# Summing the squares of a 2048-wide norm: from TensorE, group by group, to GpSimd in place with one product with the ones behind the last group

## The chip, the cores and the metric

The kernel runs on one core of a Trainium2 chip. The time is the device time of one execution in microseconds (us); the time before the change is 2414.93 us, the median of 3 runs (2414.13 to 2415.9). Everything is float32, and a float32 product takes two records of TensorE in the trace for each matmul of the code.

## The reference

Two layers of an encoder over 256 tokens of width 1024: differential attention and a bidirectional Mamba2 mixer beside each other, then a feed-forward part that fetches 128 experts' rows per token from HBM. The change touches one line of it, the norm behind the mixer (cut to what matters):

```python
y = (y_fwd + y_bwd + d_skip[:, None] * xs).reshape(b, s, SSM_INNER)   # SSM_INNER = 2048
return rmsnorm(y * jax.nn.silu(z), norm_g)          # then m @ w_ssm_br[l]

def rmsnorm(x, g):
    y = xf * lax.rsqrt(jnp.mean(xf * xf, axis=-1, keepdims=True) + RMS_EPS)
```

So the mean of the squares of 2048 features is wanted for each of 256 tokens.

## The kernel before

Each engine's program is written out by hand, in order, with semaphores between engines; no scheduler moves anything. In the stage that matters features lie on the 128 partitions and tokens along the free axis. The 2048 features are 16 tiles of 128 x 256, worked in 8 groups of two tiles, g = 0 to 7. For each group TensorE does, in this order: `beside(g + 1)`, half a chunk of the projection of z or of a gate (16 matmuls, L407); `c_times_b(g + 1)` (2 matmuls, L533); then, behind the semaphore `m_ready`, the 24 matmuls that give y of the group (L576); and from g = 2 on `sum_squares(g - 2)` (L554), two matmuls that multiply the squares with a 128 x 128 matrix of ones. They add up over the partitions, and over all 16 tiles in bank 7.

Beside it VectorE makes the differences of the decay matrices (L1166) and multiplies them with C times B (L1173 to L1182, which raises `m_ready`), adds the skip term to y and multiplies with silu(z) (L1189, L1194, which raises `yz_ready`), and scales z by the gain (L1199). ScalarE makes the exponentials (L821, L833), empties the half's bank (L815 or L794, in `aside`), and squares the group's two tiles with one instruction into `xbc` (L854, which raises `ysq_ready`), 512 elements on each partition. GpSimd only issues DMAs here: 16 loads of `fbuf`, two per group, into three slots (L1425). The load n is issued when the differences and the exponentials that used load n - 3 are done.

Behind the last group come `beside(9)`, the sums of groups 6 and 7, and the product of z with `w_ssm_br` (L392, 4 chunks of 32 matmuls each), which waits for three things: the chunk, the last scaling, and the last half's bank being emptied by ScalarE (`bank_empty`, L794). VectorE takes bank 7 (L1220), makes 1/rms of it with ScalarE's root (L875, L1224) and multiplies it into the second gates (L1225), which are first wanted when the first chunk's product is done (L1228). GpSimd's next work in the layer is fetching the experts' rows (L1443).

Of the kernel before, what the change touches and what calls it, by code (L numbers as in the profile page):

```python
# [16 lines left out]
ALU = mybir.AluOpType  # L17
# [3 lines left out]
DEPTH, SEQ, DM = 2, 256, 1024  # L21
# [8 lines left out]
XT = INNER // P  # L30
# [85 lines left out]
def encoder_kernel(nc, x, positions, consts, params, w_stream, w_dt, keys_t, norm2_rows, final_row,  # L116
                   peer_uv, out):
    with ExitStack() as ctx:
# [122 lines left out]
        def sem(name, per_layer):  # L241
            return Count(once(name), per_layer)
# [58 lines left out]
        ysq_ready = sem("ysq_ready", XT // 2)  # L301
        ysq_used = sem("ysq_used", XT // 2)
        yms_ready = sem("yms_ready", 1)
# [56 lines left out]
        def _(pe):  # L360
# [5 lines left out]
            for L in range(DEPTH):  # L366
# [183 lines left out]

                def sum_squares(g):
                    wait(ysq_ready, g + 1, L)
                    for u in range(2):
                        ins = pe.matmul(bank[7][:, 0:SEQ], ones, xbc[:, 2 * g + u, :],  # L554
                                        start=(g == 0 and u == 0), stop=(g == GROUPS - 1 and u == 1))
                    ins.then_inc(ysq_used.sem, 1)

                beside(0)
                for g in range(GROUPS):
# [19 lines left out]
                    ins.then_inc(y_done.sem, 1)  # L579
                    if g >= 2:  # L580
                        sum_squares(g - 2)
                beside(GROUPS + 1)
                sum_squares(GROUPS - 2)
                sum_squares(GROUPS - 1)
                wait(m_scaled, GROUPS, L)
# [378 lines left out]
        def _(dve):  # L964
# [32 lines left out]
            for L in range(DEPTH):  # L997
# [220 lines left out]

                wait(ysq_used, GROUPS, L)
                dve.tensor_scalar(r_bc[:], bank[7][:, 0:SEQ], 1.0 / INNER, EPS, ALU.mult, ALU.add)\  # L1220
# [184 lines left out]
        def _(pool):  # L1405
# [5 lines left out]
            for L in range(DEPTH):  # L1411
# [3 lines left out]
                pool.wait_ge(rows_stored.sem, rows_stored.at(L, 16))  # L1415
                wait(bank_full, M_ATT + 4, L)
                for n in range(F_UNITS):
                    g, d = divmod(n, 2)
                    if n >= 3:
                        gf, df = divmod(n - 3, 2)  # L1420
                        pool.wait_ge(diff_ready.sem, diff_ready.at(L, 4 * gf + 2 * df + 2))
                        pool.wait_ge(offexp_done.sem, offexp_done.at(L, 2 * gf + df + 1))
# [3 lines left out]
                                   rows_dram[L:L + 1, row:row + HPG, :].rearrange("o r t -> o (r t)")  # L1426
                                   .broadcast_to([P, HPG * TB * P])).then_inc(f_loaded[slot], 16)

                for p in range(TB * PARTS):
# [105 lines left out]
```

## Time and profile before

| | |
|---|---|
| median of 3 runs | 2414.93 us |
| the profiled execution: its time, its span | 2413.57 us, 2411.8 us |
| TensorE matmuls busy | 2081.5 us, 86% of the span |
| VectorE, ScalarE busy | 1327.4 us (55%), 749.5 us (31%) |
| the stage of the 8 groups | about 340 to 443 us in layer 0, 1534 to 1637 us in layer 1 |
| TensorE's granted clock in that stage | 1.00 of full speed |

The busy share of an engine is an average over stages with different limits; the chain of waits, cut to a stretch, says what ends last in that stretch. "PEld" is the loading of weights into TensorE, which runs ahead of the matmuls ("PE").

### The profile page before, as it was taken

Reading aid. Unit: us, or ns where it says so; the run is one execution under the profiler, and the core shown is the slowest. Engines: PE = TensorE matmul, PEld = TensorE weight load, DVE = VectorE, ACT = ScalarE, POOL = GpSimd, SP = SyncE. Lnnn points to the kernel's source line nnn. Section 1 sums busy time; section 2 is a strip of 40 time slices with the busy share of each in tenths; the row PEclk is TensorE's granted clock in tenths of the full one; section 3 lists DMA queues with packets and bytes.
Section 4 is the critical chain, followed back from the end, with each engine's and each line's share of the span. In section 5 each row is a group of like instructions: output and inputs, shape, how many; then the busy total and the mean of one; then the engine's idle time right before and its main releaser. Section 6 shows DMA issues by size and latency. Waiting matters only on the chain.

```text
span 2411.8 us, 23144 instructions
## 1 busy us (share of the span) xinstructions
PE 2081.5 (86%) x8312; PEld 1328.7 (55%) x8312; DVE 1327.4 (55%) x3225; ACT 749.5 (31%) x2017; POOL 513.4 (21%) x550
## 2 busy tenths in 40 slices
PE   5999999999878787777789999999998888777776
PEld 5688888866334332222276888888653344322322
DVE  1266458226657666765403772671366667666744
ACT  2034237103333233233220442570123332333232
POOL 0000000004334333333200000000133333333331
PEclk9999999999999999999999999999999999999999
DMA  4323444549999999999813234445499999999996
GB/s 155 135 105 140 156 172 163 201 165 373 422 422 421 422 421 421 421 421 421 370 70 134 111 140 167 166 158 201 178 387 421 421 421 421 421 422 421 422 421 268
DMA packets 90402, 705.31 MB, mean 292 GB/s; under 512 B 10000, under 2 KB 10128, under 8 KB 15792
## 3 DMA queue, kind: packets, MB, share of 16 engines
q0 software_dynamic: 78400, 553.81, 55.7%
q1 hardware_dynamic: 11168, 146.36, 15.8%
q10 hardware_dynamic: 720, 3.67, 0.5%
q8 instruction: 65, 1.06, 0.2%
q14 instruction: 49, 0.40, 0.0%
HBM read 702.62 MB, written 1.18 MB: 292 GB/s over the span
## 4 chain that ended last, share of the span: by engine, by line
PE 52%; DMA 32%; DVE 7%; ACT 4%; issue 2%; POOL 2%; SPq 0%; DVEq 0%; POOLq 0%; ACTq 0%
DMA ring<-in_peer_uv,ex_i 31%; PE bank L407 23%; PE bank L687 11%; PE bank L392 7%; DVE ring L1361 5%; PE bank L434 2%; POOL ring L1443 2%; PE bank L576 2%; PE bank L595 2%; PE bank L628 1%; ACT diag L926 1%; PE bank L554 1%; ACT wgt L919 1%; PE bank L481 1%; PE bank L533 1%
## 5 line engine op out<-in xcount | busy, mean ns | idle before, releaser
L687 PE MATMUL bank<-ring,diag 128*128 128x512 f32 x2048 | 949.7, 608 | 263.8 <-ACT diag L926 263.7
L1361 DVE SCALAR_TENSOR_TENSOR ring<-ring,h 128x1024 f32<-128x1024 f32 x512 | 607.1, 1223 | 478.4 <-DMA ring<-in_peer_uv,ex_i 478.4
L687 PEld LDWEIGHTS bank<-ring,diag 128*128 128x128 f32 x2048 | 373.2, 191 | 812.2 <-ACT diag L926 432.2
L1443 POOL DMA_INDIRECT ring<-in_peer_uv,ex_i x512 | 494.5, 966 | 1066.9 <-PE bank L687 686.3
L407 PE MATMUL bank<-hT,w_ring 128*128 128x256 f32 x2560 | 567.1, 381 | 1.9 <-ACT hT L718 1.9
L407 PEld LDWEIGHTS bank<-hT,w_ring 128*128 128x128 f32 x2560 | 485.1, 191 | 72.7 <-issue 5.3
L913 ACT ACTIVATE gel<-act_u 128x2 f32<-128x2 f32 x256 | 52.0, 203 | 854.9 <-DVE ring L1361 854.9
L926 ACT ACTIVATE diag<-cst,wgt 128x128 f32<-128x128 f32 x512 | 177.5, 394 | 25.8 <-PE bank L687 17.7
L919 ACT ACTIVATE wgt<-gel,gate_w 128x1 f32<-128x1 f32 x512 | 123.0, 287 | 9.3
L1414 POOL DMA_DIRECT2D cs_rows_dram<-cs_rows x2 | 1.3, 662 | 583.2 <-DVE cs_rows L1129 583.2
L1084 DVE SCALAR_TENSOR_TENSOR c_tmp<-xbc,par_all,c_tmp 128x254 f32<-128x254 f32 (+1 forms) x256 | 112.4, 481 | 4.5
L392 PE MATMUL bank<-zT,w_ring 128*128 128x256 f32 x512 | 110.8, 379 | 0.0
L392 PEld LDWEIGHTS bank<-zT,w_ring 128*128 128x128 f32 x512 | 97.3, 190 | 13.2
L1034 DVE TENSOR_TENSOR rot_tmp<-bank,sin_t 128x512 f32<-128x512 f32 x16 | 11.1, 692 | 142.8 <-PE bank L426 141.5
L628 PEld LDWEIGHTS bank<-hT,wq 128*128 128x128 f32 x512 | 60.0, 192 | 11.2 <-issue 9.2
L628 PEld LDWEIGHTS bank<-hT,w_ring 128*128 128x128 f32 x512 | 60.0, 192 | 8.6 <-issue 8.6
L1425 POOL DMA_DIRECT2D fbuf<-cs_rows_dram x32 | 17.4, 543 | 213.1 <-ACT m_mat L833 168.9
L628 PE MATMUL bank<-hT,wq 128*128 128x128 f32 x512 | 60.7, 276 | 1.6 <-ACT hT L882 1.6
L628 PE MATMUL bank<-hT,w_ring 128*128 128x128 f32 x512 | 60.1, 275 | 0.0
L1082 DVE TENSOR_SCALAR c_tmp<-xbc,par_all 128x256 f32<-128x256 f32 x64 | 23.4, 408 | 63.6 <-ACT xbc L767 63.6
L707 ACT ACTIVATE xn<-x_tok 128x1024 f32<-128x1024 f32 x10 | 10.5, 1051 | 153.4 <-DVE x_tok L1239 142.8
L392 PE MATMUL bank<-attT,w_ring 128*128 128x256 f32 x256 | 55.8, 380 | 2.4 <-ACT attT L805 2.4
(192 smaller groups left out, 1680.3 us busy)
## 6 DMA issues: line engine op xcount, KB each, us to landing
w_ring<-in_w_stream SPq DMA_DIRECT2D x62, 2048.0 KB, 8.3
fbuf<-cs_rows_dram POOLq DMA_DIRECT2D x32, 512.0 KB, 4.9
wq<-in_w_stream SPq DMA_DIRECT2D x4, 2048.0 KB, 8.2
ring<-in_peer_uv,ex_i POOLq DMA_INDIRECT x512, 14.5
out<-in_w_stream SPq DMA_DIRECT2D x2, 2048.0 KB, 12.2
keys<-in_keys_t ACTq DMA_DIRECT2D x2, 1024.0 KB, 4.9
x_tok<-in_x SPq DMA_DIRECT2D x1, 1024.0 KB, 5.1
g2row<-in_norm_rows ACTq DMA_DIRECT2D x2, 512.0 KB, 6.2
```

Of the source, the lines that this page charges most:

```text
L392: ins = pe.matmul(two(b0 + j // 2)[:, j % 2, :], w[:, k, j * P:(j + 1) * P], rhs(k), start=(k == 0), stop=(k == ks - 1))
L407: ins = pe.matmul(two(m % 2)[:, j % 2, :], w[:, k, j * P:(j + 1) * P], hT[:, k, :], start=(k == 0), stop=(k == KD - 1))
L434: ins = pe.matmul(bank[m % 2][:], hT[:, k, b * P:(b + 1) * P], w[:, k, :], start=(k == 0), stop=(k == KD - 1))
L576: ins = pe.matmul(two(5 + p)[u * SP_:(u + 1) * SP_, j, l * P:(l + 1) * P], xs[:, s, h * SP_:(h + 1) * SP_], m_mat[:, p, t, r, :], start=(n ...
L628: ins = pe.matmul(to[:, j * P:(j + 1) * P], w[:, k, j * P:(j + 1) * P], hT[:, k, b * P:(b + 1) * P], start=(k == 0), stop=(k == KD - 1))
L687: ins = pe.matmul(bank[b0 + n][:], diag[:, PAIR * (m % 2) + s, :], ring[:, slot, DM + n * 512:DM + (n + 1) * 512], start=False, stop=True, ...
L913: act.activation(gel[:, b, j:j + PAIR], act_u[:, b, j:j + PAIR], ACT.Gelu).then_inc(gelu_done.sem, 1)
L919: ins = act.activation(wgt[:, b, j + s:j + s + 1], gel[:, b, j + s:j + s + 1], ACT.Copy, scale=gates[:, j + s:j + s + 1])
L926: ins = act.activation(diag[:, PAIR * (m % 2) + s, :], ident, ACT.Copy, scale=wgt[:, b, j + s:j + s + 1])
L1084: ins = dve.scalar_tensor_tensor(out=dst, in0=src, scalar=w, in1=dst, op0=ALU.mult, op1=ALU.add)
L1361: ins = dve.scalar_tensor_tensor(out=row, in0=row, scalar=1.0, in1=h2[:, b, :], op0=ALU.mult, op1=ALU.mult, accum_out=act_u[:, b, PAIR * k ...
L1443: pool.indirect_dma_start(ring[:, PAIR * q + s, :], None, peer_uv, bass.IndirectOffsetOnAxis(ap=ex_i[:, b, j:j + 1], axis=0))\
```

## The change

Squares are no longer multiplied with the ones group by group. GpSimd adds the two tiles of squares of group g, as one instruction of 128 x 512, onto those of group 0, in place, for g = 1 to 7. The additions of groups 1 and 2 stand between its loads of `fbuf`, ahead of load 12 and of load 14; those of groups 3 to 7 behind the last load. TensorE multiplies the two summed tiles with the ones once, behind `beside(9)`, and waits for the seventh addition.

```diff
--- before.py
+++ after.py
@@ -299,7 +299,8 @@
         y_done = sem("y_done", GROUPS)
         yz_ready = sem("yz_ready", GROUPS)
         ysq_ready = sem("ysq_ready", XT // 2)
-        ysq_used = sem("ysq_used", XT // 2)
+        ysq_added = sem("ysq_added", GROUPS - 1)
+        ysq_used = sem("ysq_used", 1)
         yms_ready = sem("yms_ready", 1)
         yrms_ready = sem("yrms_ready", 1)
         m_scaled = sem("m_scaled", GROUPS)
@@ -548,13 +549,6 @@
                 def beside(n):
                     half(C_Z + 1 + n // 2, n % 2, M_Z + 2 + n)
 
-                def sum_squares(g):
-                    wait(ysq_ready, g + 1, L)
-                    for u in range(2):
-                        ins = pe.matmul(bank[7][:, 0:SEQ], ones, xbc[:, 2 * g + u, :],
-                                        start=(g == 0 and u == 0), stop=(g == GROUPS - 1 and u == 1))
-                    ins.then_inc(ysq_used.sem, 1)
-
                 beside(0)
                 for g in range(GROUPS):
                     p = g % 2
@@ -577,11 +571,11 @@
                                                     xs[:, s, h * SP_:(h + 1) * SP_], m_mat[:, p, t, r, :],
                                                     start=(n == 0), stop=(n == 2))
                     ins.then_inc(y_done.sem, 1)
-                    if g >= 2:
-                        sum_squares(g - 2)
                 beside(GROUPS + 1)
-                sum_squares(GROUPS - 2)
-                sum_squares(GROUPS - 1)
+                wait(ysq_added, GROUPS - 1, L)
+                for u in range(2):
+                    ins = pe.matmul(bank[7][:, 0:SEQ], ones, xbc[:, u, :], start=(u == 0), stop=(u == 1))
+                ins.then_inc(ysq_used.sem, 1)
                 wait(m_scaled, GROUPS, L)
                 wait(bank_empty, M_GSSM + 4, L)
                 for c in range(4):
@@ -1216,7 +1210,7 @@
                 scaled(GROUPS - 2)
                 scaled(GROUPS - 1)
 
-                wait(ysq_used, GROUPS, L)
+                wait(ysq_used, 1, L)
                 dve.tensor_scalar(r_bc[:], bank[7][:, 0:SEQ], 1.0 / INNER, EPS, ALU.mult, ALU.add)\
                     .then_inc(yms_ready.sem, 1)
                 wait(yrms_ready, 1, L)
@@ -1414,8 +1408,18 @@
                 pool.dma_start(rows_dram[L], cs_rows[0:2 * SH].rearrange("p b l -> p (b l)")).then_inc(rows_stored.sem, 16)
                 pool.wait_ge(rows_stored.sem, rows_stored.at(L, 16))
                 wait(bank_full, M_ATT + 4, L)
+                def add_squares(g):
+
+                    wait(ysq_ready, g + 1, L)
+                    if g > 1:
+                        pool.wait_ge(ysq_added.sem, ysq_added.at(L, g - 1))
+                    pool.tensor_tensor(xbc[:, 0:2, :], xbc[:, 0:2, :], xbc[:, 2 * g:2 * g + 2, :], ALU.add)\
+                        .then_inc(ysq_added.sem, 1)
+
                 for n in range(F_UNITS):
                     g, d = divmod(n, 2)
+                    if d == 0 and g >= 6:
+                        add_squares(g - 5)
                     if n >= 3:
                         gf, df = divmod(n - 3, 2)
                         pool.wait_ge(diff_ready.sem, diff_ready.at(L, 4 * gf + 2 * df + 2))
@@ -1425,6 +1429,8 @@
                     pool.dma_start(fbuf[:, slot].rearrange("p r b l -> p (r b l)"),
                                    rows_dram[L:L + 1, row:row + HPG, :].rearrange("o r t -> o (r t)")
                                    .broadcast_to([P, HPG * TB * P])).then_inc(f_loaded[slot], 16)
+                for g in range(3, GROUPS):
+                    add_squares(g)
 
                 for p in range(TB * PARTS):
                     b, c = divmod(p, PARTS)
```

TensorE's program of layer 0, in the middle of the loop (behind y of group 2; the names are the tiles that are written and read), before and after:

```order
L576 MATMUL bank<-m_mat,x_fwd 64x128 x2
L554 MATMUL bank<-xbc,cst 128x256 [waits ysq_ready]
L554 MATMUL bank<-xbc,cst 128x256
L407 MATMUL bank<-hT,w_ring 128x256 [waits bank_empty,chunk_loaded1]
L407 MATMUL bank<-hT,w_ring 128x256 x15
```

```order
L570 MATMUL bank<-m_mat,x_fwd 64x128 x2
L408 MATMUL bank<-hT,w_ring 128x256 [waits bank_empty,chunk_loaded1]
L408 MATMUL bank<-hT,w_ring 128x256 x15
```

The two matmuls and their wait are gone; this happens at six places in each layer.

TensorE's program behind the last group, before and after:

```order
L407 MATMUL bank<-hT,w_ring 128x256 [waits bank_empty]
L407 MATMUL bank<-hT,w_ring 128x256 x15
L554 MATMUL bank<-xbc,cst 128x256 [waits ysq_ready]
L554 MATMUL bank<-xbc,cst 128x256
L554 MATMUL bank<-xbc,cst 128x256 [waits ysq_ready]
L554 MATMUL bank<-xbc,cst 128x256
L392 MATMUL bank<-zT,w_ring 128x256 [waits chunk_loaded0,bank_empty,m_scaled]
```

```order
L408 MATMUL bank<-hT,w_ring 128x256 [waits bank_empty]
L408 MATMUL bank<-hT,w_ring 128x256 x15
L577 MATMUL bank<-xbc,cst 128x256 [waits ysq_added]
L577 MATMUL bank<-xbc,cst 128x256
L393 MATMUL bank<-zT,w_ring 128x256 [waits chunk_loaded0,bank_empty,m_scaled]
```

Two matmuls of four stay, and the wait is now for GpSimd's addition.

GpSimd's program of layer 0, from the loads of `fbuf` to the first fetch of experts, before and after:

```order
L1425 DMA fbuf<-cs_rows_dram 128x1024 [waits offexp_done,diff_ready] x13
L1443 DMA ring<-in_peer_uv,ex_i 128x2048 [waits experts_ready]
```

```order
L1429 DMA fbuf<-cs_rows_dram 128x1024 [waits offexp_done,diff_ready] x9
L1416 ISA
L1416 TENSOR_TENSOR xbc<-xbc 128x512 [waits ysq_ready]
L1429 DMA fbuf<-cs_rows_dram 128x1024 [waits offexp_done,diff_ready] x2
L1416 TENSOR_TENSOR xbc<-xbc 128x512 [waits ysq_added,ysq_ready]
L1429 DMA fbuf<-cs_rows_dram 128x1024 [waits offexp_done,diff_ready] x2
L1416 TENSOR_TENSOR xbc<-xbc 128x512 [waits ysq_added,ysq_ready] x5
L1449 DMA ring<-in_peer_uv,ex_i 128x2048 [waits experts_ready]
```

The seven additions stand where the code has them. One more instruction, of the kind ISA, stands ahead of the first of them; it is there once in the program, in layer 0, and not in layer 1.

## Rows read from the trace of the kernel before

**Rows 1.** The page's engines: busy us, share of the span, instructions.

```profile
PE 2081.5 (86%) x8312; PEld 1328.7 (55%) x8312; DVE 1327.4 (55%) x3225; ACT 749.5 (31%) x2017; POOL 513.4 (21%) x550
```

**Rows 2.** Chain of waits, 330 to 460 us: start us, us, what.

```profile
by line: PE bank L407 58.7%; PE bank L576 17.1%; PE bank L392 12.8%; PE bank L554 6.2%; PE bank L533 5.3%
...
352.43 2.77 PE bank L576 x48
...
363.16 2.77 PE bank L576 x48
...
376.67 1.06 PE bank L554 x4
377.73 6.91 PE bank L407 x32
...
388.27 1.06 PE bank L554 x4
...
441.79 1.73 PE bank L554 x8
```

**Rows 3.** Chain of waits, 1530 to 1660 us, the same stage of layer 1.

```profile
1635.90 1.73 PE bank L554 x8
```

**Rows 4.** TensorE's loading of weights, 440 to 445 us: start us, us, engine, what.

```profile
441.41 1.70 PEld L554 LDWEIGHTS bank<-xbc,cst 128*128 128x128 f32 x8
443.13 1.92 PEld L392 LDWEIGHTS bank<-zT,w_ring 128*128 128x128 f32 x9
```

**Rows 5.** ScalarE, 425 to 460 us; in brackets idle before and who ended it.

```profile
431.81 0.63 ACT L854 ACTIVATE xbc<-zT 128x512 f32<-128x512 f32 x1
435.50 0.63 ACT L854 ACTIVATE xbc<-zT 128x512 f32<-128x512 f32 x1 [3.06 <-DVE zT L1194]
...
442.19 0.47 ACT L794 ACTIVATE gateT<-bank,par_all 128x256 f32<-128x256 f32 x1
...
442.72 1.28 ACT L875 ACT_TABLE_LOAD   x1
```

**Rows 6.** ScalarE and the weight load behind it, 286 to 293 us.

```profile
289.20 2.42 ACT L805 ACTIVATE attT<-bank,subg 128x512 f32<-128x512 f32 x4 [1.59 <-PE bank L508]
...
291.68 1.38 PEld L392 LDWEIGHTS bank<-attT,w_ring 128*128 128x128 f32 x7 [1.44 <-ACT attT L805]
```

**Rows 7.** VectorE, 386 to 413 us.

```profile
401.23 1.22 DVE L1182 TENSOR_TENSOR m_mat<-m_mat,cbm 128x1024 f32<-128x1024 f32 x1
...
405.36 0.69 DVE L1194 TENSOR_TENSOR zT<-zT,xbc 128x512 f32<-128x512 f32 x1
...
408.75 0.42 DVE L1173 TENSOR_TENSOR cbm<-bank,cst 128x256 f32<-128x256 f32 x1 [1.13 <-PE bank L533]
```

**Rows 8.** TensorE, 340 to 445 us: the first of a group's y.

```profile
408.64 0.44 PE L576 MATMUL bank<-m_mat,x_fwd 128*64 128x128 f32 x4
```

**Rows 9.** GpSimd's issues, 200 to 520 us.

```profile
381.64 0.54 POOL L1425 DMA_DIRECT2D fbuf<-cs_rows_dram  x1 [4.30 <-DVE m_mat L1166]
388.40 0.54 POOL L1425 DMA_DIRECT2D fbuf<-cs_rows_dram  x1 [6.22 <-ACT m_mat L833]
...
404.84 0.54 POOL L1425 DMA_DIRECT2D fbuf<-cs_rows_dram  x1 [4.30 <-DVE m_mat L1166]
```

**Rows 10.** ScalarE, 400 to 444 us.

```profile
401.20 1.27 ACT L833 ACTIVATE m_mat<-fbuf,off_b 128x128 f32<-128x128 f32 x4
...
412.52 0.61 ACT L854 ACTIVATE xbc<-zT 128x512 f32<-128x512 f32 x1
```

**Rows 11.** The page's DMA issues: KB each, median us from issue to landing.

```profile
fbuf<-cs_rows_dram POOLq DMA_DIRECT2D x32, 512.0 KB, 4.9
ring<-in_peer_uv,ex_i POOLq DMA_INDIRECT x512, 14.5
```

**Rows 12.** VectorE, 425 to 460 us.

```profile
444.46 1.75 DVE L1224 RECIPROCAL r_bc<-r_bc 128x256 f32<-128x256 f32 x1 [0.49 <-ACT r_bc L875]
...
457.43 0.69 DVE L1228 TENSOR_TENSOR s_tmp<-bank,gateT 128x512 f32<-128x512 f32 x1 [8.89 <-PE bank L392]
```

## The prediction

> **What bounds the kernel now.** I read the page's engines first, then the chain of waits cut to the stage of the eight groups, then the timelines of each engine there. TensorE is busy 86% of the span and GpSimd 21% [rows 1], but that average decides nothing; the chain does. From 330 to 460 us it holds TensorE's lines alone, L554, the sums of squares, with 6.2% of the stretch [rows 2]. No other engine and no DMA is on it, so time taken off TensorE there comes off the end, until another engine is late. What follows the stage (the product with w_ssm_br, the routing, the fetches of experts) waits for what TensorE hands on and not for a clock, so I let it move forward as a whole.
>
> **What is removed.** Twice the stage shows what a pair of these matmuls costs. From y of group 0 to y of group 1, without L554 between, it is 363.16 - 352.43 = 10.73 us; from one pair of L554 to the next it is 388.27 - 376.67 = 11.60 us [rows 2]. The difference is 0.87 us. The 8 records of the last two pairs take 1.73 us, 0.216 each, in layer 0 and in layer 1 alike [rows 2, 3], so 4 records, a pair, are 0.865 us. The row with 1.06 us includes 0.2 us for starting on other weights behind y, which the next half will pay instead. Six pairs go from the loop: 6 x 0.865 = 5.19 us per layer.
>
> **Behind the last group** two pairs become one. That frees 0.865 us of TensorE, but something else is then last. The product L392 waits for the bank that ScalarE empties, and that row ends at 442.19 + 0.47 = 442.66 [rows 5]. Elsewhere a load of weights that waited for ScalarE began at 291.68, when the row in front of it ended at 289.20 + 2.42 = 291.62: 0.06 us later [rows 6]. The weights of L392 would then begin at 442.72, in place of 443.13 [rows 4]. So this pair gives 0.41 us and not 0.87; the other 0.45 turns into a wait for ScalarE.
>
> Sum: 5.19 + 0.41 = 5.60 us per layer, 11.2 us in both.
>
> **What is added on GpSimd.** The trace has no addition on GpSimd. Its nearest rows are the same shape on VectorE, 0.69 us for 128x512 with two inputs [rows 7], and VectorE's slowest elementwise row, 1.75 us for 256 elements, which is 3.5 us for 512 [rows 12]. I take 1.4 us, twice the nearer one, and keep 0.69 and 3.5 as ends. The Trainium skill (GPSIMD Engine Reference, section 3.1) gives 4497 ns for an addition of 2048 float32 elements on this engine; a quarter of that would be an estimated 1.1 us, and the sum would be the same.
>
> The first two additions stand between loads. GpSimd is free from 381.64 + 0.54 = 382.18 until the load at 388.40, and the last load ends at 404.84 + 0.54 [rows 9]; behind that only the additions remain. At 3.5 us each they fit, and a load that is late has room: the one issued at 388.40 lands about 4.9 us later [rows 11], at 393.3, and its first user starts at 401.20 [rows 10], 7.9 us later.
>
> The wait for the seventh addition is the one that TensorE can feel. Queued behind it is the product L392, and so all the rest. The squares of group 7 end at 435.50 + 0.63 = 436.13 [rows 5]. TensorE comes to its sum, with the pair in front of the half gone, at 441.41 - 0.87 = 440.54 on the same time scale [rows 4]. So the last addition may take 4.4 us, or the last two, from the end of group 6's squares at 431.81 + 0.63 [rows 5], 4.05 us each. Both ends of the range are below this. Price in the sum: 0. The numbers of bank 7 are wanted late as well: VectorE's gate product waits 8.89 us for TensorE's first chunk [rows 12].
>
> **VectorE and ScalarE in a shorter loop.** A group will take 10.73 us and no longer 11.60. VectorE waits 1.13 us per group for C times B [rows 7], so it keeps 1.13 - 0.87 = 0.26 us. That is nearly a second bound, but being late there is not yet a stall: the matrices that VectorE ends at 401.23 + 1.22 = 402.45 [rows 7] are wanted at 408.64 [rows 8], 6.2 us later, 5.3 in the shorter loop. Price: 0.
>
> A rule speaks against the change at this point. Before's rows can't show it, since GpSimd only issues DMAs there. The Trainium skill (SBUF — State Buffer, section "Who interferes with whom") says that VectorE and GpSimd share one pair of ports, and that an instruction of VectorE with two inputs in SBUF, or in a two-port mode, and a GpSimd instruction that reads SBUF shut each other out for their whole length. By that rule VectorE falls behind by up to one addition's length per addition; what that does to the time is the first rival.
>
> **The instruction of kind ISA** ahead of the first addition of layer 0 is in the program and in no row. I bound it from below with ScalarE's table load, 1.28 us [rows 5], and from above with the longest wait for a DMA on this queue's rows, 14.5 us [rows 11]. GpSimd is free for 388.40 - 382.18 = 6.2 us there, and the load behind it has 7.9 us: with an addition of 1.4 us, 6.2 + 7.9 - 1.4 = 12.7 us pass before anyone waits, and 12.7 + 5.3 = 18 us before TensorE does. I take 4.3 us, the middle of the two in ratio, at a price of 0. The same page of the Trainium skill (section 2.1) says that the first call of newly loaded GpSimd code pays about 6 us with no instruction visible; by that the sum would stay as it is.
>
> **Forecast.** The profiled execution took 2413.57 us; 2413.57 - 11.2 = 2402.4. The median of the runs is 1.4 us above the profiled one, so the median after is 2414.93 - 11.2 = 2403.7 us.
>
> **Rival 1: VectorE is held up by the additions.** Four additions (groups 1 to 4: the squares of the fourth end at 412.52 + 0.61 [rows 10]) fall before VectorE's last matrices. With T for one, VectorE ends up 4T late, less some 4 x 0.26 = 1 us it makes up, and TensorE feels what is beyond 5.3 us: 4T - 6.3. That is nothing up to T = 1.6 us. At T = 2.3 us it is 2.9 us a layer, and the gain falls to 5.4 us: 2409.5 us. For it: VectorE's small reserve of 0.26 us. Against it: the nearest row, 0.69 us.
>
> **Rival 2, slower: the same mechanism with a slow addition.** At T = 3.5 us VectorE costs TensorE 4 x 3.5 - 6.3 = 7.7 us per layer against 5.6 gained: 2.1 x 2 = 4.2 us slower, 2419.1 us. It decides from T = 3.0 us. For it: GpSimd would have to be five times slower than VectorE on the same shape. Against it: so slow a row is known only of the reciprocal.
>
> **Rival 3: the ISA instruction is long.** Up to 18 us nothing is lost, beyond that its excess once, in layer 0. At 24 us it is 6 us: 2409.7 us. Against it: nothing in the trace on this engine takes as long, and layer 1 doesn't have it.
>
> **Rival 4: the pairs were filling gaps, and nothing moves.** Then it stays at 2414.9 us. For it: VectorE's and ScalarE's chain would have to be as long as 11.60 us. Against it: the groups without L554 already run in 10.73 us, though VectorE has no scaling to do in the first of them.
>
> **Chances.** Forecast 0.70, rival 1 0.12, rival 2 0.06, rival 3 0.06, rival 4 0.06. A measurement of this kernel can tell about 0.2%, 4.8 us, from no change. Faster by more: the forecast, and most of rivals 1 and 3: 0.84. Within: rival 4 and the ends of 1 and 3: 0.09. Slower: rival 2 and a little of 3: 0.07. For the range, the lower end is all 14 matmuls of both layers at full price, 12.1 us, and half a microsecond of scatter between runs: 2402.2. The upper end takes in most of rivals 1 and 3: 2409.5 us.
>
> **What would show it.** In the profile after, a group of the loop takes 10.73 us in the chain and that chain still holds TensorE alone; VectorE's wait for C times B shrinks from 1.13 to about 0.26 us; four records of the product with the ones remain per layer, and the load of weights behind them waits about 0.4 us for ScalarE. Wrong would be: VectorE rows on `m_mat` longer than before while GpSimd adds, y waiting for `m_mat`, TensorE's sum waiting for GpSimd's addition, or the load of `fbuf` behind the ISA instruction landing after 401 us.

## The result and the profile after

The changed kernel takes 2401.66 us (median of 6 runs, 2396.92 to 2402.7); the kernel before, with the runs made beside it, 2414.02 us (6 runs, 2411.89 to 2415.9). The ratio is 0.9945, with a 95% interval of 0.9932 to 0.9958: 10 to 16 us faster. (A ratio here is the one on record with its interval, and not exactly the quotient of the two medians, which would be 0.9949.) Two more comparisons gave 0.9933 (0.9919 to 0.9947) and 0.9943 (0.9930 to 0.9957) on one chip and a third 0.9938 (0.9925 to 0.9952) on another. The forecast was 2403.7 us with a range of 2402.2 to 2409.5; the time lies 0.5 us below the range. The profiled execution has a span of 2396.2 us.

The chain of waits of the stage after, as in [rows 2] (start us, us, what):

```profile
by line: PE bank L408 59.5%; PE bank L393 17.6%; PE bank L570 17.1%; PE bank L534 5.3%; PE bank L577 0.7%; issue 0.1%
...
352.13 2.77 PE bank L570 x48
...
362.87 2.77 PE bank L570 x48
...
384.35 2.77 PE bank L570 x48
...
395.09 2.77 PE bank L570 x48
...
429.21 7.10 PE bank L408 x32
436.31 0.86 PE bank L577 x4
437.18 0.11 issue
437.29 22.90 PE bank L393 x105
```

It still holds TensorE alone. A group with the squares behind it took 11.60 us [rows 2] and takes 395.09 - 384.35 = 10.74 us, as the first group always did. From the first y to the product with `w_ssm_br` TensorE's timeline has these ends, first of the kernel before and then after, one line per end:

```profile
352.36 0.44 PE L576 MATMUL bank<-m_mat,x_fwd 128*64 128x128 f32 x4
...
443.35 1.89 PE L392 MATMUL bank<-zT,w_ring 128*128 128x256 f32 x8
```

```profile
352.06 0.44 PE L570 MATMUL bank<-m_mat,x_fwd 128*64 128x128 f32 x4
...
437.29 3.04 PE L393 MATMUL bank<-zT,w_ring 128*128 128x256 f32 x13
```

That is 90.99 us before and 85.23 after, 5.76 us less; in layer 1 the two lengths are the same to 0.01 us. So the stage gives 11.5 us in both layers. I call it "the stage" below. What lies behind it, in layer 0 up to the first matmul of layer 1 and in layer 1 up to the start of the last copy of x out of the banks, summed over both layers, I call "the part behind".

GpSimd after, from its tenth load of `fbuf` on, which answers to [rows 9] (start us, us, engine, what, idle before):

```profile
381.34 0.53 POOL L1429 DMA_DIRECT2D fbuf<-cs_rows_dram  x1 [4.31 <-DVE m_mat L1160]
381.98 1.27 POOL L1416 TENSOR_TENSOR xbc<-xbc 128x512 f32<-128x512 f32 x1
387.25 0.57 POOL L1429 DMA_DIRECT2D fbuf<-cs_rows_dram  x1 [4.01 <-ACT m_mat L827]
...
410.34 2.20 POOL L1416 TENSOR_TENSOR xbc<-xbc 128x512 f32<-128x512 f32 x1 [5.68 <-ACT xbc L848]
421.83 2.20 POOL L1416 TENSOR_TENSOR xbc<-xbc 128x512 f32<-128x512 f32 x1 [9.29 <-ACT xbc L848]
427.91 1.27 POOL L1416 TENSOR_TENSOR xbc<-xbc 128x512 f32<-128x512 f32 x1 [3.88 <-ACT xbc L848]
431.60 1.26 POOL L1416 TENSOR_TENSOR xbc<-xbc 128x512 f32<-128x512 f32 x1 [2.42 <-ACT xbc L848]
```

An addition takes 1.27 us, and 2.20 us in two of the seven. The last one ends at 432.86, and TensorE comes for it at 436.15, 3.3 us later. An instruction named MODIFY_POOL_CONFIG is in the trace as well, just ahead of the first addition, where the program has the ISA instruction (there as one, here as two records):

```profile
L1416 POOL TENSOR_TENSOR xbc<-xbc x14: 1265/1277/2205, 382.0 to 1620.0; 128x512 f32<-128x512 f32 x14
L1416 POOLq MODIFY_POOL_CONFIG  x2: 37/37/37, 381.9 to 381.9; - x2
```

A record takes 37 ns, and the addition behind it starts 0.11 us after the load in front ended. VectorE's rows beside the additions (the first beside GpSimd's row at 381.98, the second and third beside the two of 2.20 us):

```profile
381.87 1.94 DVE L1188 TENSOR_TENSOR zT<-zT,xbc 128x512 f32<-128x512 f32 x1
...
411.33 1.62 DVE L1193 TENSOR_SCALAR zT<-zT,par_all 128x256 f32<-128x256 f32 x2
...
422.82 1.62 DVE L1193 TENSOR_SCALAR zT<-zT,par_all 128x256 f32<-128x256 f32 x2
```

The product with silu(z) took 0.69 us [rows 7] and takes 1.94, longer by one addition. The two gain scalings took 0.61 us and take 1.62. The additions of 2.20 us began 0.14 us behind the start of a VectorE row of 1.22 us (410.20 and 410.34 for the first of them). It ends at 412.54, 1.1 us behind the end of that row, about the length of an addition. VectorE and GpSimd do shut each other out, as the Trainium skill (SBUF — State Buffer, "Who interferes with whom") says; but TensorE never waits for it.

### The profile page after: what moved, and what is told of

The parts are those of the page before. It is cut to its first block, busy times and chain, and to the rows that moved or that the text cites. A ratio compares the mean times of both kernels' runs of the same rounds, so it can differ in the third digit from the quotient of the medians.

```text
span 2396.2 us, 23060 instructions
## 1 busy us (share of the span) xinstructions
PE 2070.5 (86%) x8256; PEld 1317.2 (55%) x8256; DVE 1339.8 (56%) x3225; ACT 749.8 (31%) x2017; POOL 539.2 (23%) x564
## 4 chain that ended last, share of the span: by engine, by line
PE 52%; DMA 32%; DVE 8%; ACT 4%; issue 2%; POOL 2%; SPq 0%; DVEq 0%; POOLq 0%; ACTq 0%
DMA ring<-in_peer_uv,ex_i 31%; PE bank L408 23%; PE bank L681 11%; PE bank L393 7%; DVE ring L1355 5%; PE bank L435 2%; POOL ring L1449 2%; PE bank L570 2%; PE bank L589 2%; PE bank L622 1%; ACT diag L920 1%; ACT wgt L913 1%; PE bank L482 1%; PE bank L534 1%; PE bank L427 1%
## 5 line engine op out<-in xcount | busy, mean ns | idle before, releaser
L920 ACT ACTIVATE diag<-cst,wgt 128x128 f32<-128x128 f32 x512 | 177.5, 394 | 18.7 <-PE bank L681 10.4
L622 PEld LDWEIGHTS bank<-hT,wq 128*128 128x128 f32 x512 | 60.0, 192 | 11.2 <-issue 9.2
```

The lines of the kernel that those rows point to most:

```text
L622: ins = pe.matmul(to[:, j * P:(j + 1) * P], w[:, k, j * P:(j + 1) * P], hT[:, k, b * P:(b + 1) * P], start=(k == 0), stop=(k == KD - 1))
L920: ins = act.activation(diag[:, PAIR * (m % 2) + s, :], ident, ACT.Copy, scale=wgt[:, b, j + s:j + s + 1])
```

## The experiments

Each kernel was run in rounds beside the kernel before on the same chip. Eighteen runs were made on three chips, A, B and C; the kernel before has medians of 2413 to 2415 us on A and about 2419 on B and C, so times are compared only with their own kernel before. The chip of the first comparison is not on record; its times and traces look like those of A, and I count it there. The diffs are cut to what matters. Those of adds_beside, sums_twice and before_warm are against the kernel before, the others against the changed kernel.

| kernel (chip) | median us | kernel before | ratio, 95% interval | stage, layers 0 and 1 |
|---|---|---|---|---|
| after_again (A) | 2398.95 | 2414.76 | 0.9933, 0.9919 to 0.9947 | 85.22, 85.23 |
| no_adds (A) | 2400.13 | 2414.76 | 0.9935, 0.9921 to 0.9949 | 85.22, 85.23 |
| adds_beside (A) | 2413.61 | 2414.76 | 0.9996, 0.9986 to 1.0005 | 91.00, 90.99 |
| sums_twice (A) | 2426.24 | 2414.76 | 1.0040, 1.0027 to 1.0054 | 97.90, 97.89 |
| before_again (A) | 2413.27 | 2413.05 | 0.9998, 0.9989 to 1.0007 | 91.00, 90.99 |
| adds_x3 (A) | 2418.44 | 2413.05 | 1.0020, 1.0011 to 1.0029 | 93.50, 93.38 |
| vector_adds (A) | 2398.92 | 2413.05 | 0.9944, 0.9930 to 0.9957 | 85.23, 85.22 |
| tail (A) | 2400.68 | 2413.05 | 0.9943, 0.9930 to 0.9957 | 84.52, 84.52 |
| pad_3 (B) | 2405.76 | 2418.96 | 0.9946, 0.9933 to 0.9959 | 85.23, 86.25 |
| pad_6 (B) | 2407.51 | 2418.96 | 0.9951, 0.9939 to 0.9963 | 85.22, 87.54 |
| pad_10 (B) | 2409.68 | 2418.96 | 0.9961, 0.9950 to 0.9973 | 85.23, 89.26 |
| layer0_only (B) | 2408.52 | 2418.96 | 0.9964, 0.9951 to 0.9977 | 85.22, 90.99 |
| before_warm (C) | 2421.90 | 2418.70 | 1.0015, 1.0006 to 1.0024 | 90.99, 90.99 |
| after_warm (C) | 2407.57 | 2418.70 | 0.9960, 0.9946 to 0.9974 | 85.23, 85.22 |
| after_ref (C) | 2403.64 | 2418.70 | 0.9938, 0.9925 to 0.9952 | 85.23, 85.23 |
| before_pair (A) | 2412.51 | 2415.04 | 0.9996, 0.9987 to 1.0005 | 90.99, 90.99 |
| after_pair (A) | 2399.61 | 2415.04 | 0.9943, 0.9930 to 0.9957 | 85.22, 85.23 |
| vector_pair (A) | 2399.70 | 2415.04 | 0.9944, 0.9931 to 0.9958 | 85.23, 85.22 |

The stage is read from each record like the two above; it repeats to 0.02 us between records of one kernel, while whole runs of one kernel differ by 3 to 9 us. That is what makes the stage the measure of the mechanism here.

**after_again, after_ref, after_pair:** the changed kernel as it is, and **before_again, before_pair:** the kernel before as it is.

> The changed kernel once more, to size the gain and the scatter. Theory A (TensorE alone is given back time, 5.76 us in each layer's stage by the two traces, and nothing else moves): 11.5 us faster than before, ratio 0.9952. Theory B (the stage gives 11.5 us and the fetches of experts behind it gain 1 to 4 us more, as the profiled execution had it): 13 to 15 us faster, ratio 0.9938 to 0.9946.

> The kernel before against itself: ratio 1.000; what its interval and its runs span is what a comparison can tell. If the fetches of experts vary from run to run by some us (theory of scatter), the runs span 3 us or more while the stage of the groups takes 90.99 us per layer in its trace too.

The gain is there in each of the three comparisons, 15 to 16 us by the medians and 14 to 16 by the ratios, and the kernel before against itself gives 1.000. The stage's 0.9952 lies outside the interval of after_again by a little and at the edge of that of after_ref, so theory B (something behind the stage as well) had to be followed.

**no_adds** leaves out the additions (the norm's sum then holds group 0 alone):

```diff
-                def add_squares(g):
...
-                    if d == 0 and g >= 6:
-                        add_squares(g - 5)
...
-                for g in range(3, GROUPS):
-                    add_squares(g)
...
-                wait(ysq_added, GROUPS - 1, L)
+                wait(ysq_ready, GROUPS, L)
```

> The changed kernel without GpSimd's additions: TensorE multiplies only group 0's squares with the ones, behind group 7's squares, so the norm's sum leaves out groups 1 to 7. Theory A (the additions are hidden and cost nothing): same as the changed kernel within its scatter, stage of the groups 85.2 us from y of group 0 to the product. Rival (the additions cost TensorE time through VectorE): this kernel is faster than the changed one by 1 us or more in the stage. VectorE's row L1188 should be back at 0.69 us everywhere if it was GpSimd that made it 1.9.

The stage is 85.22 us and the time that of the changed kernel within its scatter. The additions cost TensorE nothing. VectorE's product with silu(z) takes its 0.69 us again, so it was the additions that made it 1.94. And its wait for C times B in the shorter loop is 0.26 us here, as forecast; in the changed kernel the additions use that up.

**adds_beside** is the other half alone: the kernel before, TensorE's sums kept, with GpSimd's additions beside them (the first waits for TensorE's first sum).

```diff
                     wait(ysq_ready, g + 1, L)
+                    if g == 1:
+                        wait(ysq_used, 1, L)
...
                 wait(ysq_used, GROUPS, L)
+                wait(ysq_added, GROUPS - 1, L)
```

> The kernel before with GpSimd's seven additions put beside it, TensorE's sums all kept. Theory A: same as before (ratio 1.000), stage 90.99 us per layer as before, VectorE rows up to 1.2 us longer. Rival (additions cost): slower by 1 to 5 us.

Same as before, though VectorE is held up here too:

```profile
L1195 DVE TENSOR_TENSOR zT<-zT,xbc 128x512 f32<-128x512 f32 x16 | 18.2, 1138 | 0.5
```

(16 products with silu(z), 1.14 us in the mean in place of 0.69.) Together with no_adds this puts the whole of the stage's gain on TensorE's 14 matmuls.

**sums_twice** makes each pair of sums twice:

```diff
-                    for u in range(2):
-                        ins = pe.matmul(bank[7][:, 0:SEQ], ones, xbc[:, 2 * g + u, :],
-                                        start=(g == 0 and u == 0), stop=(g == GROUPS - 1 and u == 1))
+                    for v in range(4):
+                        ins = pe.matmul(bank[7][:, 0:SEQ], ones, xbc[:, 2 * g + v % 2, :],
+                                        start=(g == 0 and v == 0), stop=(g == GROUPS - 1 and v == 3))
```

> The kernel before with every pair of L554 made twice, so the sum that goes into the norm is doubled. If TensorE bounds the stage, each of 16 more matmuls per layer costs 0.432 us: 13.8 us slower in two layers, ratio 1.0057, stage 90.99 + 6.9 = 97.9 us. If the pairs partly fill gaps: less.

The stage grew to 97.90 us, 6.91 for 16 matmuls, exactly 0.432 each: TensorE bounds it from both sides. The whole grew by 11.5 us by the medians and by 9.7 by the ratio, 2 to 4 us less than both stages, with 13.8 at 1.0057 just outside the interval. I have no cause for that difference.

**adds_x3** makes each addition three times in a row:

```diff
+                    for i in range(3):
+                        if g > 1 or i > 0:
+                            pool.wait_ge(ysq_added.sem, ysq_added.at(L, 3 * (g - 1) + i))
+                        pool.tensor_tensor(xbc[:, 0:2, :], xbc[:, 0:2, :], xbc[:, 2 * g:2 * g + 2, :], ALU.add)\
+                            .then_inc(ysq_added.sem, 1)
```

> The changed kernel with each of GpSimd's additions made three times in a row (3 x 1.27 = 3.8 us a group, group 1 to 7 counted three times in the sum). Theory of the held-up VectorE: each addition shuts VectorE out for its 1.27 us, four groups before the last matrices cost VectorE 15.2 us, less 1 us reserve and 5.3 us room: TensorE waits 8.9 us per layer, the kernel is 17.8 us slower than the changed one, about 6 us slower than before. Rival (only the wait behind the last group counts): the last group's additions end 3.8 us behind its squares, 0.8 us before TensorE asks, and with those of group 6 queued ahead 1 to 4 us after: 2 to 8 us slower than the changed kernel.

It is 19.5 us above vector_adds and 5.4 above the kernel before (by the ratio 4.8): the slower rival of the prediction, brought about. Its waits in layer 0's stage (who waited for whom: us, times, longest), and the end of its chain:

```profile
PEld bank L570 <- DVE m_mat L1176: 4.3, 1, 4.3
PE bank L570 <- DVE m_mat L1176: 3.9, 1, 3.9
...
PE bank L577 <- POOL xbc L1417: 2.6, 1, 2.6
```

```profile
436.97 1.28 POOL xbc L1417
...
444.21 1.27 POOL xbc L1417
445.52 1.25 PE bank L577 x4
```

VectorE's products with C times B there; and, for TensorE, the last row of y behind the first wait and the same row a group later:

```profile
414.53 4.64 DVE L1173 TENSOR_TENSOR m_mat<-m_mat,cbm 128x512 f32<-128x512 f32 x4
```

```profile
425.18 0.65 PE L570 MATMUL bank<-m_mat,x_fwd 128*64 128x128 f32 x4
...
435.38 0.39 PE L570 MATMUL bank<-m_mat,x_fwd 128*64 128x128 f32 x4
```

Both mechanisms are there, and each of my two expectations named one way alone. VectorE's four products take 4.64 us here, where they take 2.5 without an addition beside them, and the matmuls of y stand still 3.9 us for it (the load of their weights 4.3). Then the six additions of groups 6 and 7 run from 436.97 to 445.48, and TensorE's sum waits 2.6 us for them. The stage of layer 0 is 93.50 - 85.23 = 8.3 us longer. Most of the 1.8 us that these two waits leave is the clock. Behind the first wait it fell to 0.50 (from 422 to 426 us its mean is 0.57), and y of that group took from 421.43 to 425.76, 4.33 us for 2.77. In layer 1 the clock stayed at 1.00 up to the sum. There TensorE waited 3.8 and 0.5 us for VectorE and 3.7 for GpSimd, and the stage is as long to 0.12 us. That fits the chain, in which the six additions come last: the slower y of layer 0 made TensorE's wait for them shorter and the stage no longer.

**vector_adds, vector_pair** take the additions from GpSimd and put them on VectorE behind each group's scaling:

```diff
                     ins.then_inc(m_scaled.sem, 1)
+                    if g > 0:
+                        if g > 1:
+                            wait(ysq_added, g - 1, L)
+                        dve.tensor_tensor(xbc[:, 0:2, :], xbc[:, 0:2, :], xbc[:, 2 * g:2 * g + 2, :], ALU.add)\
+                            .then_inc(ysq_added.sem, 1)
```

> The additions on VectorE, behind each group's scaling, in place of GpSimd. VectorE gets 0.69 us more per group where GpSimd's additions held it up by 0.9 to 1.2 us. Theory: its reserve of 0.27 us is overdrawn by 0.42 us per group, 2.5 us over six groups, inside the 5.3 us of room: same as the changed kernel. Rival (VectorE's reserve is what counts): 2 to 5 us slower than the changed kernel, still faster than before.

The stage is the same, 85.23 us, and so is the time. VectorE's room of 5.3 us covers the 0.69 us per group as it covers the time that GpSimd's additions shut it out. Which of the two engines adds makes no difference here.

**tail** shortens the end of the stage:

```diff
-                wait(ysq_added, GROUPS - 1, L)
-                for u in range(2):
-                    ins = pe.matmul(bank[7][:, 0:SEQ], ones, xbc[:, u, :], start=(u == 0), stop=(u == 1))
+                wait(ysq_added, GROUPS, L)
+                ins = pe.matmul(bank[7][:, 0:SEQ], ones, xbc[:, 0, :], start=True, stop=True)
...
-                wait(bank_empty, M_GSSM + 4, L)
+                wait(bank_empty, M_GSSM + 3, L)
                 for c in range(4):
+                    if c == 1:
+                        wait(bank_empty, M_GSSM + 4, L)
...
+                wait(ysq_added, GROUPS - 1, L)
+                pool.tensor_tensor(xbc[:, 0, :], xbc[:, 0, :], xbc[:, 1, :], ALU.add).then_inc(ysq_added.sem, 1)
```

> The changed kernel with the end of the stage shortened: GpSimd adds tile 1 onto tile 0 as an eighth addition, TensorE makes one matmul with the ones (0.43 us) and not two, and the product's first chunk waits for the bank of the half before and not for the last half's, which only its second chunk overwrites. Expected: 0.43 + 0.28 us gained per layer, 1.1 to 1.4 us in all against the changed kernel, which is at the edge of what 5 rounds can tell; the stage in the trace 84.5 us in place of 85.2. If the eighth addition is late: a wait of TensorE for GpSimd, no gain.

The stage is 84.52 us, 0.71 less, as worked out. In the time it doesn't show: 2400.68 us beside vector_adds at 2398.92.

### What lies behind the stage

In the first pair of records the spans differ by 15.6 us, and the stages by 11.5. In both, TensorE pauses where a layer's expert part begins, and here is where they part (granted clock and DMA share are the third and second number from the right of each line; first before, then after, in layer 1, each from the pause on):

```profile
1757.46:1761.46 4.00, 0.99 (x4) 1.02 (x5) 3.34 (x15) 1.86 (x6) 1.51 (x2) 0.79 1.01 424
1761.46:1765.46 4.00, 4.00 (x9) 2.20 (x9) 3.62 (x13) 1.28 (x4) 0.00 (x0) 0.50 1.01 426
1765.46:1769.46 4.00, 4.00 (x9) 1.71 (x8) 3.50 (x9) 0.00 (x0) 0.00 (x0) 0.85 0.62 260
1769.46:1773.46 4.00, 4.00 (x10) 1.71 (x9) 3.05 (x9) 1.41 (x6) 2.52 (x2) 1.00 0.46 113
```

```profile
1745.70:1749.70 4.00, 2.09 (x11) 1.57 (x12) 3.33 (x14) 2.30 (x7) 1.56 (x2) 1.00 1.01 426
1749.70:1753.70 4.00, 4.00 (x10) 1.71 (x9) 2.53 (x11) 0.69 (x3) 0.00 (x0) 1.00 1.01 418
1753.70:1757.70 4.00, 4.00 (x11) 1.81 (x10) 3.06 (x7) 1.34 (x5) 2.27 (x3) 1.00 1.02 418
1757.70:1761.70 4.00, 4.00 (x11) 1.80 (x10) 3.02 (x7) 0.73 (x3) 2.45 (x3) 1.00 0.98 389
```

Before, TensorE's clock stands at 0.50 for a while, 1.2 of 2.4 GHz, behind a pause of 3.7 us, and 4 us later the DMA engines run half empty. After, neither happens in layer 1; in layer 0 both have the fall. In all 13 records of chip A the fall at this place takes 3.4 us in a layer, or 6.8, or doesn't come. Ordered by its time over both layers:

| time at 0.50 | records: part behind the stage, us | mean |
|---|---|---|
| 0 | no_adds 1534.0, vector_adds 1532.0, vector_pair 1531.7 | 1532.6 |
| 3.4 us | after 1533.6, after_again 1532.6, adds_x3 1536.5 | 1534.2 |
| 6.8 us | before_again 1536.6, before_pair 1536.7, adds_beside 1535.6, tail 1536.4, after_pair 1535.4 | 1536.1 |
| 10.2 us | before 1537.0, sums_twice 1538.3 | 1537.6 |

The longer the clock is down, the longer the part behind, by some 1.7 us for each 3.4, and the kernels with a stage of 85.23 us have it less often: their six records have a part behind of 1531.7 to 1535.4 us, the four with a stage of 90.99 us one of 1535.6 to 1537.0. Two things are not in the table. adds_x3 has two more falls of 3.4 us behind the end of its stages, one in each layer, and would stand with them in the last row. And every record has more falls later in the expert part, 22 to 44 us in all, which go with the part behind only weakly. That the two go together is no cause; three trials were to show whether it is one.

**pad_3, pad_6, pad_10** delay layer 1 of the changed kernel:

```diff
                 wait(ysq_added, GROUPS - 1, L)
+                for _ in range(3 if L == 1 else 0):
+                    pe.matmul(bank[7][:, 0:SEQ], ones, xbc[:, 0, :], start=True, stop=True)
```

> The changed kernel with three more products with the ones, of which nothing is kept, ahead of its sum in layer 1 alone: the product L393 of layer 1 starts 3 x 0.432 = 1.3 us later, less the 0.28 us it waits for ScalarE anyway, 1.0 us. Theory of the clock: whether TensorE's granted clock falls to 0.50 for some 3 to 5 us at the start of layer 1's expert part hangs on when its pause of about 3 us there falls; it fell in all six records with the stage at 90.99 or 97.9 us and in one at 84.52, and not in four at 85.23. If a shift of 1 us brings the fall back, this kernel takes 1.0 us for the shift and 1 to 2 us for the fall, 2 to 3 us more than the changed one. Rival (the fetches of experts, not the clock, gave the 2 us): 1.0 us more, fall or not.

> The same with six products: shift 2.6 - 0.28 = 2.3 us. Theory of the clock: 2.3 us more than the changed kernel without the fall, 3.5 to 4.5 with it; its record shows which. Rival: 2.3 us.

> The same with ten products: shift 4.3 - 0.28 = 4.0 us. Theory of the clock: 4.0 us more without the fall, 5 to 6 with it. Rival: 4.0 us. If among the three shifts the fall comes and goes, it hangs on the time of the pause and not on the change.

The stages grew by 1.02, 2.31 and 4.03 us, as worked out, and the times step up by 1.75 and 2.17 us where the stages do by 1.29 and 1.72. But the chip was another, without a run of the changed kernel as it is and without a trace of the kernel before, on which TensorE's pause falls elsewhere (0.78 us ahead of layer 0's key scores, where it is about 2.9 on chip A). The pause ahead of the queries is the long one here, and behind it layer 1's clock fell in all three; TensorE's rows of pad_3 from 1725 to 1760 us by groups (busy us, mean ns, idle before), and the stretch:

```profile
L624 PE MATMUL bank<-hT,wq 128*128 128x128 f32 x64 | 9.0, 313 | 3.2 <-ACT hT L878 3.2
```

```profile
1742.00:1746.00 4.00, 0.79 (x8) 0.55 (x6) 3.67 (x12) 2.33 (x5) 0.50 (x1) 1.00 1.01 422
1746.00:1750.00 4.00, 4.00 (x22) 4.00 (x23) 3.48 (x14) 2.91 (x8) 0.00 (x0) 0.57 1.01 422
```

A padding of 1 to 4 us moves the whole layer, pause and all, and so it didn't make the fall come or go. The trial said nothing of what a fall costs. (pad_3's expectation counts six records with a fall in layer 1 and a stage of 90.99 or 97.9 us. They were four, and adds_x3.)

**layer0_only** makes the change in layer 0 alone:

```diff
+                    if L == 1 and g >= 2:
+                        sum_squares(g - 2)
...
-                    if d == 0 and g >= 6:
+                    if L == 0 and d == 0 and g >= 6:
```

> The change in layer 0 alone; layer 1 sums on TensorE as before. By the stage alone 5.76 us faster than before, half of the changed kernel's 11.5: ratio 0.9976. If the 1 to 4 us beyond the stage come from layer 1's clock: with the fall in layer 1's record 5 to 6 us faster than before, without it 7 to 8.

Ratio 0.9964, 8.7 us faster (by the medians 10.4) where one stage gives 5.76, with 5.76 (0.9976) at the edge of the interval. Its layer 1 had the fall, and by the expectation it should then have gained 5 to 6 us. But its layer 0 had none, so one record says little against the clock. It says something else, which I had not looked for. TensorE's queries behind the pause, in layer 0 and in layer 1:

```profile
552.66 7.41 PE L636 MATMUL bank<-hT,wq 128*128 128x128 f32 x64 [3.22 <-ACT hT L890]
```

```profile
1748.68 9.04 PE L636 MATMUL bank<-hT,wq 128*128 128x128 f32 x64 [3.21 <-ACT hT L890]
```

The pause is the same, and without the fall the queries take 1.6 us less. From the product with `w_ssm_br` to the first product with x it is 125.4 us in layer 0 and 127.0 in layer 1. The three padded kernels have the same code in layer 0, had the fall there, and took 127.0. So at this place a fall of 3.4 us costs 1.6 us up to the first product with x. That it then reaches the end of the program is not shown.

**before_warm, after_warm** fill the pause on TensorE, in both kernels:

```diff
                 query_tiles(0, 1, range(4))
+                pe.wait_ge(mix_empty.sem, mix_empty.at(L, 12))
+                for _ in range(6):
+                    pe.matmul(bank[7][:, 0:SEQ], ones, hT[:, 0, :], start=True, stop=True)
                 key_scores(0, 1)
```

> The kernel before, with six products with the ones (2.6 us, nothing of them is kept) in TensorE's pause ahead of the key scores of the second block, in both layers. Theory of the clock: the granted clock stays at 1.00 there, the key scores take 1.0 us and not 2.0, the DMA engines are idle 1 us less in each layer, 2 to 4 us faster than before: ratio 0.9983 to 0.9992. Rival (the clock's fall costs nothing, the fetches scatter by themselves): same as before or slower by up to 2 us, since the six products delay the key scores where the pause is short.

> The changed kernel with the same six products. Theory of the clock: its record had the fall in layer 0 alone, so it gains 1 to 2 us: 0 to 2 us faster than the changed kernel, and before_warm minus after_warm is the stage's 11.5 us. Rival: before_warm minus after_warm is 13 to 16 us, as in the pair without the products.

> The changed kernel on the same chip as the two above. Stage alone: 11.5 us faster than before (0.9952); with what the first comparisons had beyond it: 13 to 16 us (0.9933 to 0.9946).

Both became slower, by 3.2 and 3.9 us against their own partners, and they differ by 14.3 us and not by the stage's 11.5. The clock had still fallen in both, in an earlier pause: of before_warm TensorE's rows there are

```profile
556.62 1.04 PE L614 MATMUL bank<-cst,h 128*128 128x128 f32 x8
560.88 10.23 PE L628 MATMUL bank<-hT,wq 128*128 128x128 f32 x64 [3.22 <-ACT hT L885]
570.94 2.76 PE L673 MATMUL bank<-hT,cst 128*128 128x256 f32 x12
```

with a pause of 3.22 us in front of the queries, 0.79 us long on chip A, and the queries taking 10.23 us for 7.41. The products, 2.6 us in a layer, stood behind it and only added to the time: up to the first product with x it is 128.5 to 130.1 us, for 127.0 and 127.4 in after_ref. What the theory forecast (no fall, and a difference of 11.5 us) came in neither part. But since the fall stayed, the trial didn't make the state that the theory is about, and leaves it open.

> The kernel before against itself: ratio 1.000. In its record the part from the product behind the groups to the end of the expert part takes, by the first theory (DMA engines idle longer at the start of the expert part), 2 to 4 us more over both layers than in after_pair; by the rival (scatter alone) the same within 1 us.

> The changed kernel, same chip: 11.5 us faster by the stage alone; 13 to 16 us if the parts behind the stage are shorter too.

> The additions on VectorE, same chip: same as after_pair within 1.5 us, its first comparison having shown 2398.92 us beside 2398.95.

The last three ran on chip A again. The part behind takes 1536.7 us in before_pair, 1535.4 in after_pair and 1531.7 in vector_pair: the two kernels with the same stage are further from each other than from the kernel before, in the order of their falls (two, one twice as long, none; 6.8, 6.8 and 0 us). Their medians are the same to 0.1 us. So one record's part behind says little of a kernel's median. What stays open is why the times of the kernels with a stage of 85.23 us lie beyond the stage's 11.5 us in all seven comparisons: by 0.8 us in the first and 2.6 to 4.3 in the others by the medians, by 1.8 to 4.7 by the ratios. Each interval reaches 3 us to either side, and some of the seven share their runs of the kernel before, so they are fewer independent ones than seven; that all lie on one side speaks for something behind the stage and is no proof of it. The falls of the clock go with the part behind in the records, and one costs 1.6 us where layer0_only shows it; that they are why the medians gain more than the stage has not been shown.

## Why the prediction was right or wrong

The direction and the mechanism in the stage were right. The number, 2403.7 us, is 2.0 us above the time, and the time lies outside the range. The step that failed is the one that made the range: half a microsecond for scatter between runs, around one median of three runs. Of the 2.0 us, 0.9 are the median of the kernel before, which was 2414.93 us in three runs and is 2414.02 in six; 0.3 are the stage, 11.5 us for 11.2; the 0.8 that are left lie outside the stage. By the prediction's own steps:

- **Six pairs in the loop, 5.19 us per layer.** Right: groups of 10.74 us throughout, for 10.73 forecast.
- **The last pair, 0.41 us.** The mechanism was right and its size off. ScalarE's last row ended at 436.73 + 0.47 = 437.20, and the load of weights began at 437.26, 0.06 us behind it, as [rows 6] had it. But I carried the saving over from one load to the other, and took the matmul to follow its load by 443.35 - 443.13 = 0.22 us, as in an unbroken stream. It started 0.03 us behind it, at 437.29. The wait for ScalarE is there, 0.5 us for the 0.4 forecast. The pair gave 0.57 us, and the stage 5.76 for 5.60.
- **GpSimd's additions, price 0.** Right. They took 1.27 us, near the 1.4 I chose, and 2.20 twice, beside a VectorE row that had begun before them. no_adds and adds_beside show no cost.
- **VectorE's reserve and room.** Right as far as it was used: VectorE's wait for C times B went from 1.13 us to nothing (0.26 in no_adds), it was held up by 1.2 us beside three additions of a layer and by 1.0 beside three, and y never waited: the last matrices were done at 422.91 and wanted at 426.37. Rival 1 forecast no loss up to 1.6 us per addition. adds_x3, with 3.8 us per group, shows the loss beyond it. Rival 1's formula gives 4 x 3.8 - 6.3 = 8.9 us of waiting for VectorE there; TensorE waited 3.9 to 4.3 for VectorE, and most of what is left of the stage's 8.3 came from the last additions, which the formula left out, and in layer 0 from the clock.
- **The ISA instruction.** 37 ns; the 4.3 us I took was far too much, and it hung on nothing. The Trainium skill (GPSIMD Engine Reference, section 2.1) has about 6 us for the first call of newly loaded code; here the first addition began 0.11 us behind the load in front of it and took 1.27 us like the others. No such pause was paid in this case; whether new code was loaded at all, the trace doesn't show.
- **"I let it move forward as a whole."** This assumption had no row beside it, and the records don't bear it out. Of the 15.6 us between the first two spans 11.5 are the stage's, 3.4 lie in the part behind (1537.0 and 1533.6 us) and 0.7 elsewhere, and all comparisons of the change lie beyond 11.5 us. The part holds most of the time. Why it is shorter stays open.
- **The lower end of the range.** This step failed. It took half a microsecond for scatter. The kernel before alone runs from 2411.9 to 2415.9 us in the first comparison, its median moved by 0.9 us between 3 runs and 6, and runs of one kernel differ by 3 to 9 us in the later ones. With the stage's 11.5 us from the second median the time would be 2402.5, inside the range. Had I read the three runs of before (2414.13 to 2415.9) as a spread of 1.8 us and not as a point, the lower end would have been 2414.93 - 12.1 - 1.8 = 2401.0, and the time inside. The sum itself is off by 0.1 as well: 2414.93 - 12.1 - 0.5 is 2402.3 and not 2402.2.
- **Rival 4** (gaps were filled) is ruled out by the groups of 10.74 us, and by sums_twice: each matmul more costs its full 0.432 us in the stage.

## What to carry to other kernels

Where the chain of waits of a stage holds one engine alone, count its instructions: each one that goes or comes is paid in full, and two groups of the same stage with and without it give the price to a hundredth. Before work goes to another engine, work out how late its neighbour may become (here 5.3 us of room for VectorE) and not only its busy share; one addition of 1.27 us per group disappeared in it and three did not. And a range for the whole needs the spread of whole runs, since parts of the program that the change doesn't touch may move by more than the term that one works out to 0.1 us. A median of three runs is no fixed point either: here it moved by 0.9 us with three more.

## What the runs showed of the hardware

- A GpSimd addition of 128 x 512 float32 takes 1.27 us, against 0.69 us for VectorE's row of that shape [rows 7].
- They shut each other out. Beside an addition VectorE's row of 0.69 us takes 1.87 to 1.94. Where an addition began 0.14 us behind the start of a VectorE row of 1.22 us, it takes 2.20 us, and the scalings behind that row 1.62 for 0.61. The one that is held up isn't always the one whose row starts later: at 381.87 VectorE's row starts 0.11 us ahead of the addition and is the one that gets longer.
- The matmul whose weight load waited for ScalarE starts 0.03 us behind the start of that load (437.26 and 437.29); the same one in a running stream 0.22 (443.13 and 443.35).
- TensorE's granted clock fell from 1.00 to 0.50 in or right behind pauses of 2 to 4 us, for 3.4 or 6.8 us, in some records and not in others of the same program. In layer 0 of the changed kernel it fell behind 2.19 and 2.78 us (after_again, after) and not behind 2.92 (after_pair); other kernels have it behind 2.85 (before_pair) and not behind 2.97 and 3.72 (vector_pair, adds_x3). The key scores of a block take 2.04 us then for 1.13, and the queries 9.04 for 7.41.
- Chips differ in a stretch that no kernel changed: from the product with `w_ssm_br` to the first product with x it is 122 to 126 us on chip A and 127 on B and C (125.4 in the one layer without the fall, and without the kernels with added products), with TensorE's pause in front of the queries 0.79 us on the one and 3.2 to 3.6 on the others.
